# Norm 2 of a two-layer transformer trunk: four of the eight k tiles of the latent unit multiply tokens that the norm has not scaled yet

## The chip, the cores and the metric

The kernel runs on one core of a Trainium2 chip. Its metric is the device time in microseconds (us) of one execution; lower is better. One run is also recorded by the hardware profiler, and every row below comes from that recording. TensorE (PE) multiplies matrices, VectorE (DVE) and ScalarE (ACT) work on tiles in SBUF and PSUM, GpSimd (POOL) and SyncE (SP) mainly issue DMAs here.

## What is computed

Two layers over 256 tokens of width 1024. Each has a mixer (layer 0 sparse attention, layer 1 latent attention, MLA) and a gated feed-forward, and four times a root-mean-square norm stands between the residual stream x and a product:

```
mod = silu(c) @ ada_w[i] + ada_b[i]                  # shift, scale, gate of this layer
hm  = rms(x, norm_mix[i]) * (1 + scale) + shift      # norms 0 and 2
cq, ckv, k_rot = split(hm @ mla_w_in, [384, 640])    # layer 1: the "latent unit"
x   = x + gate * mixer(...)
hf  = rms(x, norm_ffn[i]) * (1 + scale_f) + shift_f  # norms 1 and 3
x   = x + gate_f * (silu(a) * b) @ ffn_w_out         # a, b = halves of hf @ ffn_w_in
```

Norm 2 is the one at the start of layer 1, between the down product of layer 0's feed-forward and the product with `mla_w_in`. Since a token's root is one number for all its columns, a product of normed tokens can be had as root times (x with gain and scale, times W), plus (shift times W), the same row for all tokens. That identity is what the change uses.

## The kernel before

Everything is one program per engine, with the order of the work written out by hand and semaphores between the engines. Tokens lie in T = 2 tiles of 128, the width in KD = 8 k tiles. A product in full precision is three matmuls, high by high, low weights by high tokens, high weights by low tokens (lines 1934 to 1936). So each weight slot s is loaded raw by SP, rounded by ACT into `w_hi` (`high`, line 778) and its rest is taken by DVE into `w_lo` (`low`, line 1165). A ring of RING = 4 slots is in use: slot s can be rounded when `slot_used` says that slot s - 4 was multiplied. `high_to(n)` and `low_to(n)` make all slots below n that are not made yet, in order. IN1 to IN1 + 3 are the four slots of the first latent unit (288 columns: key-value latent and rotary key), INB1 = IN1 + 4 to INB1 + 3 those of the second (384 columns: query latent). KVB1 is the first slot after them.

A norm in the old form, as norm 2 has it: DVE adds the gated down product into x in four pieces (two column halves, two token tiles; `update_x`, lines 1347 and 1355), ACT takes the squares of each (line 796), DVE makes the roots (lines 1202 to 1216) and scales both halves (`scaled_half`, line 1225). PE turns the scaled tokens in five batches (PIECES, line 1959), ACT applies scale and shift and rounds (lines 815 and 818: `st_hi`), DVE takes the rest (line 1241: `st_lo`), PE multiplies. While PE waits, `norm_start` has it multiply 42 and then 10 small filler matrices into a bank that nobody reads (line 2015, IDLE_FIRST and IDLE_SECOND).

Norms 1 and 3, ahead of the up products, already have the new form (`factored`, `early_tokens`, `first_unit`). There the first KU = 4 k tiles of x are turned before the root is known and kept in `early_hi`, `early_lo`; PE multiplies the shift row alone (`shift_hi`, `shift_lo`: the shift repeated for 128 tokens, into bank sc1) and then the early tokens; ACT copies the shift row's product; DVE folds root times early product plus shift row into `early_sums`. The other four k tiles go the old way as three batches (LATE_PIECES: tiles 4, 5, and 6 with 7), and DVE joins the two halves (line 1415). The tiles 0 to 3 are turned once more, scaled, as the last two batches of LATE_PIECES, since the following units need them in the old form.

After norm 2 DVE's list goes on as follows in both kernels: position to float (1768), angles (1771), then `low_to(KVB1)`, which makes the low parts of INB1 to INB1 + 3 if they aren't made yet, then the roots of the latents (1178 to 1196), their scaling (1793), and so on. PE's second latent unit waits for the low part of its slot before each slot.

## Time and profile before

| | us |
|---|---|
| median of 3 runs (733.5 to 735.42) | 733.95 |
| the profiled execution | 732.78 |
| its span, first to last instruction | 730.9 |
| PE busy in the span | 696.1 (95%) |
| DVE busy | 535.7 (73%) |
| ACT busy | 380.9 (52%) |
| last matmul of the down product starts | 416.17 |
| first matmul of the second latent unit starts | 432.22 |

A timeline row reads: start in us from the span's start, duration, engine, line, operation, output and inputs with shapes, how many instructions were merged, and in brackets how long the engine had stood idle and what released it. Matmuls overlap, so the distance of two starts is the pace and the duration is not. A "windows" row gives for a stretch its length, then the busy time of PE, of its weight loads, of DVE, ACT and POOL with instruction counts, the granted TensorE clock as a share of full speed, the DMA share and GB/s.

### The profile page before, as it was taken

How to read it: one execution, taken by the hardware profiler on the slowest of the kernel's cores; microseconds unless marked ns; L12 is line 12 of the kernel's file. 1: busy time of each engine (PE TensorE's matmuls, PEld its weight loads, DVE VectorE, ACT ScalarE, POOL GpSimd, SP SyncE). 2: the span in 40 equal slices, each digit the busy share in tenths (PEclk: the TensorE clock that was granted, in tenths of full speed). 3: DMA queues.
4: the chain of work that ended last, by engine and by line, in shares of the span. 5: the costliest groups of instructions: out<-in, count | busy, mean ns of one | idle time of the engine just before them, and what ended most of it. 6: DMA issues, size and time to landing. Idle time of an engine off the chain costs nothing. (4 is left out here: it accounts for less than half of the span.)

```text
span 730.9 us, 10691 instructions
## 1 busy us (share of the span) xinstructions
PE 696.1 (95%) x3839; PEld 569.7 (78%) x3839; DVE 535.7 (73%) x1004; ACT 380.9 (52%) x714; POOL 89.5 (12%) x175
## 2 busy tenths in 40 slices
PE   3799999999999999999999999889999999999997
PEld 2577768787778888878878887768888888878886
DVE  2356697999788989987887578978778765554444
ACT  2345566576468444444333379677576454444331
POOL 8020212000020111212211100600000000000000
PEclk9999999999999999999999999999999999999999
DMA  8997996033183999998898482601537865545621
GB/s 289 348 382 209 376 359 219 1 115 89 39 280 116 354 316 349 344 343 288 289 338 297 123 224 65 231 1 59 171 101 242 287 204 176 174 171 173 212 76 58
DMA packets 93742, 155.09 MB, mean 212 GB/s; under 512 B 5979, under 2 KB 68064, under 8 KB 93696
## 3 DMA queue, kind: packets, MB, share of 16 engines
q1 hardware_dynamic: 80768, 111.24, 45.9%
q0 software_dynamic: 12928, 43.24, 17.3%
q8 instruction: 28, 0.46, 0.3%
q14 instruction: 18, 0.15, 0.1%
HBM read 151.32 MB, written 1.05 MB: 208 GB/s over the span
## 5 line engine op out<-in xcount | busy, mean ns | idle before, releaser
L778 ACT ACTIVATE w_hi<-raw 128x1024 fp32r<-128x1024 f32 (+3 forms) x198 | 200.8, 1024 | 252.0 <-PE lin L1936 228.2
L1165 DVE TENSOR_TENSOR w_lo<-raw,w_hi 128x1024 fp32r<-128x1024 f32 (+3 forms) x198 | 233.0, 1186 | 110.6 <-ACT w_hi L778 110.0
L1934 PE MATMUL lin<-w_hi,st_hi 128*128 128x512 f32 (+2 forms) x552 | 220.0, 398 | 2.3 <-DVE w_lo L1165 2.0
L1936 PE MATMUL lin<-w_hi,st_lo 128*128 128x512 f32 (+2 forms) x552 | 212.6, 385 | 0.0
L1935 PE MATMUL lin<-w_lo,st_hi 128*128 128x512 f32 (+2 forms) x552 | 211.9, 384 | 0.0
L1934 PEld LDWEIGHTS lin<-w_hi,st_hi 128*128 128x128 f32 x552 | 104.1, 189 | 27.4 <-issue 5.2
L1936 PEld LDWEIGHTS lin<-w_hi,st_lo 128*128 128x128 f32 x552 | 103.9, 188 | 20.6
L1935 PEld LDWEIGHTS lin<-w_lo,st_hi 128*128 128x128 f32 x552 | 104.3, 189 | 18.6 <-issue 0.7
L634 POOL DMA_DIRECT2D ada_ring<-in_ada_w_dram x80 | 42.7, 534 | 384.0 <-DVE acc L1302 299.7
L1302 DVE SCALAR_TENSOR_TENSOR acc<-ada_ring,cond_b,acc 128x1024 f32<-128x1024 f32 x64 | 81.9, 1280 | 2.1 <-DMA ada_ring<-in_ada_w_dram 2.0
L1934 PE MATMUL lin<-w_hi,hid_hi 128*128 128x512 f32 x176 | 70.2, 399 | 0.2 <-DVE hid L1401 0.2
L1936 PE MATMUL lin<-w_hi,hid_lo 128*128 128x512 f32 x176 | 68.9, 392 | 0.0
L1935 PE MATMUL lin<-w_lo,hid_hi 128*128 128x512 f32 x176 | 68.5, 389 | 0.0
L1936 PEld LDWEIGHTS lin<-w_hi,hid_lo 128*128 128x128 f32 x176 | 33.0, 188 | 7.7
L1934 PEld LDWEIGHTS lin<-w_hi,hid_hi 128*128 128x128 f32 x176 | 33.1, 188 | 7.4 <-DVE hid L1401 0.6
L1935 PEld LDWEIGHTS lin<-w_lo,hid_hi 128*128 128x128 f32 x176 | 33.1, 188 | 7.2 <-issue 0.2
L866 ACT ACTIVATE z<-z,nmax 128x128 f32<-128x128 f32 x64 | 28.4, 445 | 14.3 <-DVE nmax L1378 14.3
L815 ACT ACTIVATE tfull<-tp,ada_cols,scale_cols 128x256 f32<-128x256 f32 x32 | 16.5, 557 | 12.3 <-issue 7.1
L1241 DVE TENSOR_TENSOR st_lo<-tfull,st_hi 128x512 fp32r<-128x512 f32 (+1 forms) x22 | 13.3, 607 | 12.2 <-ACT st_hi L818 11.9
L1347 DVE TENSOR_TENSOR scratch<-lin,gate_rows 128x512 f32<-128x512 f32 x16 | 11.0, 689 | 11.8 <-PE lin L1936 11.7
L1959 PE MATMUL tp<-ident,z 128*128 128x128 f32 x96 | 16.4, 281 | 3.4 <-ACT prob_t L874 3.4
L796 ACT ACTIVATE scratch<-x 128x512 f32<-128x512 f32 x16 | 10.0, 625 | 16.3 <-DVE x L1355 13.2
(295 smaller groups left out, 892.3 us busy)
## 6 DMA issues: line engine op xcount, KB each, us to landing
raw<-in_ffn_w_in_dram SPq DMA_DIRECT2D x88, 512.0 KB, 5.1
ada_ring<-in_ada_w_dram POOLq DMA_DIRECT2D x80, 512.0 KB, 6.2
raw<-in_ffn_w_out_dram SPq DMA_DIRECT2D x22, 1024.0 KB, 5.6
raw<-in_nsa_w_in_dram SPq DMA_DIRECT2D x10, 1024.0 KB, 12.7
ada_first<-in_ada_w_dram SPq DMA_DIRECT2D x8, 1024.0 KB, 13.0
raw<-in_nsa_cmp_w_dram SPq DMA_DIRECT2D x4, 1024.0 KB, 10.6
raw<-in_nsa_w_out_dram SPq DMA_DIRECT2D x4, 1024.0 KB, 9.6
raw<-in_mla_w_out_dram SPq DMA_DIRECT2D x4, 1024.0 KB, 5.5
```

Of the source, the lines that this page charges most:

```text
L634: pool.dma_start(ada_ring[:, n % ARING, :], ada_source(a)).then_inc(ada_landed[n % ARING], 16)
L778: nc.scalar.activation(part_of(w_hi, s), raw_part(s), ACT.Copy).then_inc(hi_ready, 1)
L815: ins = nc.scalar.activation(dst, src, ACT.Identity, scale=scale[:, k:k + 1], bias=shift[:, k:k + 1])
L866: e = nc.scalar.activation(prob_b[:, n % 3, c0:c0 + w], prob_b[:, n % 3, c0:c0 + w], ACT.Exp, bias=nmax[:, n % 4, t:t + 1], scale=-1.0, ac ...
L1165: nc.vector.tensor_tensor(part_of(w_lo, s), raw_part(s), part_of(w_hi, s).bitcast(F32), ALU.subtract).then_inc(lo_ready, 1)
L1241: nc.vector.tensor_tensor(low[:, k0:k0 + nk, :], tfull[:, m % 2, 0:nk * S].rearrange("p (k s) -> p k s", k=nk), high[:, k0:k0 + nk, :].bit ...
L1302: nc.vector.scalar_tensor_tensor(total, ada_ring[:, n % ARING, :], cond_b[:, kt, 0:1], total, ALU.mult, ALU.add).then_inc(acc_summed, 1)
L1347: ins = nc.vector.tensor_tensor(tmp, lin[2 * (unit % 2) + t][:], gate_rows[:, row, 512 * n:512 * n + 512], ALU.mult)
L1934: nc.tensor.matmul(bank, a_h, w_h, start=first, stop=False)
L1935: nc.tensor.matmul(bank, a_h, w_l, start=False, stop=False)
L1936: return nc.tensor.matmul(bank, a_l, w_h, start=False, stop=last)
L1959: ins = nc.tensor.transpose(tp[batch % 2][0:rows, n * P:(n + 1) * P], src, ident[:])
```

## The change

Norm 2 takes the form of norms 1 and 3. The fillers at norm 2 go. Buffers of its own (`mid_hi`, `mid_lo`, `mid_sum`) hold its shift, since the usual ones lie over a part of `hid_lo` that the last down products still read. The first latent unit becomes a shift product (12 matmuls of 288 columns), early products for tiles 0 to 3 (24) and late products for tiles 4 to 7 (24). Its sum is now written to `proj1` by DVE (the join), and ACT squares it there; ACT's two copies of this unit go. The low parts of IN1 and IN1 + 1 are moved into the middle of the last x update. POOL's two DMAs that fill the unused rows of the query and key tiles wait for the join and no longer for the down product, as they would write over the early tokens. The second latent unit waits for the last two batches of tokens. Norms 1 and 3 only change names.

```diff
-T_H1 = _batches(len(PIECES), "st")
+T_XM = _batches(2, "st")
+T_H1 = _batches(len(LATE_PIECES), "st")
...
-            pool.wait_ge(slot_used, IN1)
+            pool.wait_ge(halves_joined, 2 * T)
...
# ACT
-            before_norm(DOWN0 + FK, 2)
-            modulated(2, T_H1, 6)
+            shift_split(2, 6)
+            squares_of_x(2, 0)
+            high_to(IN1 + 2)
+            squares_of_x(2, 1, [0])
+            early_high(2, T_XM, 0)
+            squares_of_x(2, 1, [1])
+            early_high(2, T_XM, 1)
+            high_to(IN1 + 4)
+            modulated(2, T_H1, 6, LATE_PIECES, 0, 2)
+            shift_sum_copied(2, KVL + ROT)
+            modulated(2, T_H1, 6, LATE_PIECES, 2)
...
                     bank = lin[2 * ((U_IN1 + u) % 2) + t]
+                    if u == 0:
+                        act.wait_ge(halves_joined, T + t + 1)
+                        bank = proj1[:, t, c0:c0 + n]
...
-                    ev = nc.scalar.activation(proj1[:, t, c0:c0 + n], bank[:, 0:n], ACT.Copy)
+                    if u == 1:
+                        ev = nc.scalar.activation(proj1[:, t, c0:c0 + n], bank[:, 0:n], ACT.Copy)
...
# DVE
+            shift_low(2, 6)
             update_x(U_DOWN0, 1, 0, (part_done, 2))
-            update_x(U_DOWN0 + 1, 1, 1, (slot_used, DOWN0 + FK), 3)
-            low_to(DOWN0 + FK + 1)
-
-
-            normalise_x()
-            modulated(IN1)
+            update_x(U_DOWN0 + 1, 1, 1, (slot_used, DOWN0 + FK), 3, lambda: low_to(IN1 + 2))
+            early_low(0)
+            roots_of_x()
+            early_low(1)
+            factored(2, IN1, U_IN1, KVL + ROT)
+            for k0, nk in LATE_PIECES[3:]:
+                scaled_low(k0, nk)
+            dve.wait_ge(slot_used, INB1)
+            dve.wait_ge(early_folded, 2)
+            for t in range(T):
+                nc.vector.tensor_tensor(proj1[:, t, QL:MLA_IN], early_sums[t][:, 0:KVL + ROT],
+                                        lin[2 * (U_IN1 % 2) + t][:, 0:KVL + ROT], ALU.add).then_inc(halves_joined, 1)
...
# PE
+            def early_product(norm, unit0, s0, n, tp_x, t, k):
+
+                cols = slice(t * P, (t + 1) * P)
+                pe.wait_ge(resid, 4 * (norm - 1) + T + t + 1)
+                pe.wait_ge(st_ready, stationary_number(tp_x) + k // 2 + 1)
+                ins = half_product(lin[2 * ((unit0 - 1) % 2) + t], s0, n,
+                                   (early_hi[:, k, cols], early_lo[:, k, cols]), k, 0)
+                if t == T - 1 and k % 2 == 1:
+                    ins.then_inc(slot_used, 1)
+
+            def late_products(norm, unit0, s0, n, tp_h):
+
+                wait_unit(unit0)
+                for k in range(KU, KD):
+                    pe.wait_ge(lo_ready, s0 + k // 2 + 1)
+                    if k < KD - 1:
+                        pe.wait_ge(st_ready, stationary_number(tp_h) + k - KU + 1)
+                        x_batch(tp_h, k - KU + 2)
+                    for t, sides in enumerate(stationary(k)):
+                        ins = half_product(lin[2 * (unit0 % 2) + t], s0, n, sides, k, KU)
+                    if k % 2 == 1:
+                        ins.then_inc(slot_used, 1)
+                pe.wait_ge(early_folded, norm)
...
-            norm_start(T_H1, 10, IDLE_FIRST)
-            unit(U_IN1, IN1, FOUR, KVL + ROT, stationary, st_wait(T_H1, x_batch))
+            early_tokens(2, T_XM)
+            shift_product(2, IN1, KVL + ROT, 10)
+            for q in range(2):
+                for t in range(T):
+                    for k in (2 * q, 2 * q + 1):
+                        early_product(2, U_IN1, IN1, KVL + ROT, T_XM, t, k)
+            for m in range(2):
+                x_batch(T_H1, m)
+            late_products(2, U_IN1, IN1, KVL + ROT, T_H1)
...
             def key_value_latent(k):
 
+                if k in (0, 2):
+                    pe.wait_ge(st_ready, stationary_number(T_H1) + 4 + k // 2)
```

`factored` is unchanged but for its arguments: scale columns 512 to 1023 of x; low part of slot s + 2; rests of the batches with tiles 4 and 5; low part of slot s + 3; root; scale columns 0 to 511; wait for the shift row; fold; rest of the batch with tiles 6 and 7.

## Rows read from the trace of the kernel before

**Rows 1.** The page's first part: busy time, share of span, instructions.

```profile
PE 696.1 (95%) x3839; PEld 569.7 (78%) x3839; DVE 535.7 (73%) x1004; ACT 380.9 (52%) x714; POOL 89.5 (12%) x175
```

**Rows 2.** Windows view, from the down product's end to the second latent unit.

```profile
416.40:432.22 15.82, 14.54 (x117) 13.98 (x116) 12.27 (x29) 11.62 (x22) 2.16 (x2) 1.00 0.83 193
```

**Rows 3.** Timeline of PE at norm 2.

```profile
416.17 0.40 PE L1936 MATMUL lin<-w_hi,hid_lo 128*128 128x512 f32 x1
416.40 4.85 PE L2015 MATMUL sc<-ident,ones 128*128 128x128 f32 x42
...
424.14 0.38 PE L1934 MATMUL lin<-w_hi,st_hi 128*128 128x288 f32 x1
424.36 0.30 PE L1935 MATMUL lin<-w_lo,st_hi 128*128 128x288 f32 x1
424.49 0.29 PE L1936 MATMUL lin<-w_hi,st_lo 128*128 128x288 f32 x1
...
426.98 0.63 PE L1959 MATMUL tp<-ident,scratch 128*128 128x128 f32 x4 [0.55 <-DVE st_lo L1241]
...
432.22 0.34 PE L1934 MATMUL lin<-w_hi,st_hi 128*128 128x384 f32 x1
```

**Rows 4.** Timeline of DVE at norm 2.

```profile
411.10 0.69 DVE L1347 TENSOR_TENSOR scratch<-lin,gate_rows 128x512 f32<-128x512 f32 x1 [3.75 <-PE lin L1936]
...
426.14 0.69 DVE L1241 TENSOR_TENSOR st_lo<-tfull,st_hi 128x512 fp32r<-128x512 f32 x1 [1.07 <-ACT st_hi L818]
426.75 0.75 DVE L1165 TENSOR_TENSOR w_lo<-raw,w_hi 128x576 fp32r<-128x576 f32 x1
...
429.36 0.69 DVE L1241 TENSOR_TENSOR st_lo<-tfull,st_hi 128x512 fp32r<-128x512 f32 x1 [0.96 <-ACT st_hi L818]
...
430.58 3.68 DVE L1165 TENSOR_TENSOR w_lo<-raw,w_hi 128x768 fp32r<-128x768 f32 x4
```

**Rows 5.** Timeline of ACT at norm 2.

```profile
412.55 0.63 ACT L796 ACTIVATE scratch<-x 128x512 f32<-128x512 f32 x1 [7.69 <-DVE x L1355]
...
426.01 1.00 ACT L815 ACTIVATE tfull<-tp,ada_cols,scale_cols 128x256 f32<-128x256 f32 x2
...
427.64 1.02 ACT L815 ACTIVATE tfull<-tp,ada_cols,scale_cols 128x256 f32<-128x256 f32 x2
```

**Rows 6.** Timeline of PE at norm 1, which has the new form.

```profile
213.27 0.39 PE L1936 MATMUL lin<-w_hi,st_lo 128*128 128x512 f32 x1
...
218.79 0.50 PE L1934 MATMUL lin<-w_hi,early_hi 128*128 128x512 f32 x1
...
220.29 0.60 PE L1959 MATMUL tp<-ident,scratch 128*128 128x128 f32 x4
...
225.53 0.63 PE L1959 MATMUL tp<-ident,scratch 128*128 128x128 f32 x4
```

**Rows 7.** Timeline of DVE at norm 1.

```profile
221.81 0.43 DVE L1241 TENSOR_TENSOR st_lo<-tfull,st_hi 128x256 fp32r<-128x256 f32 x1 [1.15 <-ACT st_hi L818]
222.72 0.42 DVE L1241 TENSOR_TENSOR st_lo<-tfull,st_hi 128x256 fp32r<-128x256 f32 x1 [0.48 <-ACT st_hi L818]
223.06 1.22 DVE L1165 TENSOR_TENSOR w_lo<-raw,w_hi 128x1024 fp32r<-128x1024 f32 x1
...
224.39 0.88 DVE L1225 TENSOR_SCALAR scratch<-x,stat 128x512 f32<-128x512 f32 x2
225.19 0.74 DVE L1268 SCALAR_TENSOR_TENSOR silu_a<-lin,stat,shift_sum 128x512 f32<-128x512 f32 x1
```

**Rows 8.** Timeline of PE after the first pauses of the kernel.

```profile
21.16 1.09 PE L1959 MATMUL tp<-ident,scratch 128*128 128x128 f32 x4 [2.09 <-DVE st_lo L1241]
...
24.18 0.63 PE L1936 MATMUL lin<-w_hi,st_lo 128*128 128x512 f32 x1
24.61 0.57 PE L1934 MATMUL lin<-w_hi,st_hi 128*128 128x512 f32 x1
```

**Rows 9.** Timeline of PE at the start of the key-value product.

```profile
441.40 0.50 PE L1934 MATMUL lin<-w_hi,st_hi 128*128 128x512 f32 x1 [0.23 <-DVE st_lo L1241]
```

More of the change, by code:

```diff
@@ L1264, in factored @@
                 scaled_half(0)
[L1265 removed]
+                dve.wait_ge(shift_copied, norm)
                 dve.wait_ge(slot_used, s + 2)
                 for t in range(T):
[L1268 to L1269 removed]
+                    ins = nc.vector.scalar_tensor_tensor(
+                        early_sums[t][:, 0:n], lin[2 * ((unit - 1) % 2) + t][:, 0:n], root[:, t:t + 1],
+                        shifts[norm - 1][2][:, 0:n], ALU.mult, ALU.add)
                 ins.then_inc(early_folded, 1)
                 scaled_low(*LATE_PIECES[2])
[L1273 to L1279 removed]
             def low_from_tp(batch, hi, lo, i=None):
@@ L1915, in _ @@
             roots_of_x()
-            factored(1, UP1, U_UP1)
+            factored(3, UP1, U_UP1)
             def last_sums(u):
@@ L2015, in idle_into, with shift_product, half_product @@
                     nc.tensor.matmul(bank[:, 0:P], ones[:], ident[:], start=True, stop=True)
-            def norm_start(batch0, seg_read, n):
+            def shift_product(norm, s0, n, seg_read):
                 pe.wait_ge(ada_out, ada_at(seg_read))
-                idle_into(sc[1], n)
-                for m in range(2):
-                    x_batch(batch0, m)
-                idle_into(sc[1], IDLE_SECOND)
+                pe.wait_ge(shift_ready, norm)
+                hi, lo, _ = shifts[norm - 1]
+                for k in range(KU):
+                    pe.wait_ge(lo_ready, s0 + k // 2 + 1)
+                    ins = half_product(sc[1], s0, n, (hi[:, k, :], lo[:, k, :]), k, 0)
+                ins.then_inc(shift_done, 1)
+            def half_product(bank, s0, n, sides, k, first):
+                s, j = s0 + k // 2, k % 2
+                return three(bank[:, 0:n], *sides, w_hi[:, s % RING, n * j:n * j + n],
+                             w_lo[:, s % RING, n * j:n * j + n], k == first, k == first + KU - 1)
+            def early_product(norm, unit0, s0, n, tp_x, t, k):
[9 more added lines that the diff above has]
+                for k in range(KU, KD):
+                    pe.wait_ge(lo_ready, s0 + k // 2 + 1)
+                    if k < KD - 1:
[6 more added lines that the diff above has]
+                pe.wait_ge(early_folded, norm)
             def stationary(k):
@@ L2167, in feed_forward @@
                 hid0 = stationary_number(tp0)
[L2169 to L2172 removed]
                 def first_unit():
[L2176 to L2181 removed]
+                    shift_product(2 * layer + 1, up, 512, seg_read)
                     for t in range(T):
[L2183 to L2184 removed]
                         for k in range(KU):
[L2186 to L2190 removed]
+                            early_product(2 * layer + 1, unit0, up, 512, tp_x, t, k)
                         if t == 0:
@@ L2193, in first_unit @@
                                 x_batch(tp_h, m)
[L2194 to L2204 removed]
+                    late_products(2 * layer + 1, unit0, up, 512, tp_h)
                 def wait_st(k):
```

82 lines of the change are left out of this document (22 added, 60 removed).

## Prediction

> **What bounds the kernel now.** I read the page's first part, then the windows view around norm 2, then the timelines of PE, DVE and ACT there, and last those of norm 1, which already has the new form. PE is busy 95% of the span [rows 1], so outside its few pauses the kernel is as long as PE's work. Norm 2 is such a pause in disguise. The last down matmul starts at 416.17, and what follows at 416.40 are 42 filler matmuls that give nothing [rows 3]; the first useful product starts at 424.14 and the second latent unit at 432.22. Those 15.82 us hold 14.54 us of "busy" PE [rows 2], but 48 matmuls of 288 columns at a pace of 0.13 (424.36 to 424.49, [rows 3]) are only 6.4 us. The reader is to see that the rest is a chain through DVE, ACT and PE (x, squares, roots, scaling, turning, rounding, rest), and that what a change here is worth is read at one point: when the second latent unit can start.
>
> **What the change does to that chain.** Norm 1 is the ruler. Its last matmul starts at 213.27 [rows 6], that of norm 2 at 416.17, so I add 202.90 to norm 1's times as long as the work is the same, and correct where a slot has 576 columns and not 1024.
>
> Hidden at no cost: the shift's high and low parts (one ACT and one DVE instruction of 512 columns, each about the 0.63 and 0.69 of such tiles), because ACT stands idle 7.69 us before 412.55 [rows 5] and DVE 3.75 us before 411.10 [rows 4]; the 12 matmuls of the shift product (12 x 0.13 = 1.6 us), because PE has only fillers then; the low parts of IN1 and IN1 + 1, moved ahead of the last x update, which end when that update's product is there (they delay it by at most 0.1, and ACT, not DVE, is what the early tokens wait for). If that cover were gone, the two low parts would cost 2 x 0.75 [rows 4]. The ACT copies that go (two short ones) lie behind the join and aren't on the path to the second unit. POOL's two DMAs start some 16 us later; behind them on POOL stands only the rotation of queries, not due before the query unit, and SP's loads for later slots go out as the low parts are made.
>
> Now step by step:
> 1. PE's second group of early products starts at 218.79 + 202.90 = 421.69 [rows 6]. It has 12 matmuls, 0.22 for the first (424.14 to 424.36) and 0.13 for the others, 1.7 us in all [rows 3]: end 423.38. Here the shorter product is no help yet; PE turns the late tiles 4 and 5 at 423.38.
> 2. In norm 1 the rests of these two batches start 1.52 and 2.43 us after the turning at 220.29 [rows 6, 7]: 424.90 and 425.81.
> 3. From the second of them to the scaling of columns 0 to 511 norm 1 takes 224.39 - 222.72 = 1.67, which has a low part of 1.22 in it [rows 7]; here that low part takes 0.75 [rows 4], so 1.20: DVE scales at 427.01. That is the first new delay: the old kernel had both halves scaled in one go, before any turning. PE turns tiles 0 and 1 at 225.53 - 224.39 = 1.14 later [rows 6, 7]: 428.15.
> 4. ACT follows a turning after 427.64 - 426.98 = 0.66 [rows 3, 5]: 428.81; its next batch of two tiles comes 427.64 - 426.01 = 1.63 later [rows 5]: 430.44. The turning for that one (tiles 2 and 3) waits for the rest of tiles 6 and 7, which DVE makes after scaling (0.80, [rows 7]) and two folds. A fold of 288 columns has no row: at least what I take for the join below (0.37), at most the 0.74 of 512 columns [rows 7]; nearer to the first for its width, 0.43. The rest starts at 427.01 + 0.80 + 2 x 0.43 = 428.67 and the turning 426.98 - 426.14 = 0.84 after it [rows 3, 4], at 429.51, 0.3 ahead of what ACT needs (430.44 - 0.66). So ACT's pace decides, barely; with the dear folds the batch would come 0.35 later.
> 5. DVE's last rest starts 429.36 - 427.64 = 1.72 after ACT [rows 4, 5]: 432.16. In the old kernel it is at 429.36. That is 2.80 late, though the unit itself is done earlier: after that turning (four matrices at the fillers' pace of 4.85 / 42 = 0.115, [rows 3]) PE has 12 matmuls left and ends at 429.51 + 0.46 + 0.09 + 12 x 0.13 = 431.6, 0.6 before 432.22.
> 6. Then comes the new wait. **Nobody has made the low part of INB1.** The old list goes from the last rest at 429.36 to the low part at 430.58, 1.22 in all [rows 4]: the rest, the cast and the angles. The first of the four low parts takes 0.95 (3.68 in four, the last one whole), ready at 431.53, and PE got there at 432.22: a slack of 0.54 with 0.15 for the signal (426.98 - 426.14 - 0.69). The new list has the join in between. The trace shows no join of 288 columns. The nearest rows are rests of 256 columns (0.34 from start to next start, 222.72 to 223.06, [rows 7]) and of 512 (0.61, 426.14 to 426.75, [rows 4]); I take 0.37 each, close to the first: 0.74 for both, at most 1.22. It doesn't wait itself, as PE is done at 431.6.
> 7. So the low part of INB1 starts at 432.16 + 1.22 + 0.74 = 434.12, is there at 435.07, and PE starts the second unit at 435.22 in place of 432.22. **Sum: + 2.80 + 0.74 - 0.54 = + 3.00 us.** PE stands still from about 431.7 to 435.2. Queued behind the wait on PE are the second unit, the turned key-value latent and the key-value product; behind the join on DVE are the four low parts, the latent's roots and its scaling.
>
> By the Trainium skill ("VectorE: DVE Perf Modes", section on the TRN2 errata), an operand in PSUM has a fixed cost of 120 cycles and not 58, which would make the two joins 0.13 us longer, + 3.1 instead of + 3.0; the trace shows no such difference between a fold from PSUM (0.74) and other tiles of 512 columns beyond 0.05 [rows 4, 7].
>
> **Does it stay?** Later pauses of PE end on DVE and ACT work that itself hangs on this unit: the key-value product starts at 441.40 after a wait of 0.23 for a rest of the latent [rows 9], which hangs on the turning inside the second unit. DVE's own list moves by 2.80 + 0.74 = 3.5 up to the low parts, and what follows on it waits for the same unit's squares and turnings. All three engines move together, and loads are released by low parts, with no fixed date. Nothing gives it back.
>
> **Rivals.**
> A, as above: + 3.0. Its own range: the step 4 tie, the join's bounds (0 to + 0.5), and 0.5 for the ruler: + 2.2 to + 3.9. Chance 0.62.
> B, the clock falls. With the fillers gone PE pauses some 1.7, 1.3 and 3.5 us in 12 us. For it: after the kernel's first pauses (2.09 us before 21.16) matmuls of 512 columns start 0.43 apart (24.18 to 24.61), against 0.23 at norm 2 (416.17 to 416.40), so these ran at 1.2 GHz and not at 2.4 [rows 3, 8]. Against it: the slow stretch lies at the very start, the pauses to come follow 400 us of steady work, and the granted clock at norm 2 is 1.00 now [rows 2]. Price: slow from 21.16 to 24.61 [rows 8], 3.45 us x (1 - 0.23 / 0.43) loses 1.6. Total + 4.6, up to + 5.5 if it falls twice. The Trainium skill ("TensorE: Matmul & The Clock Gate", section "Why this matters for your kernels") tells one to leave no longer idle gaps between bursts of matmuls, since the clock falls back; by that rule this would be the likely case, and no row after the start shows it. Chance 0.20.
> C, the low part of INB1 doesn't bind, because DVE and ACT fall behind less than the ruler says. Then PE's own end at 431.6 sets the start: - 0.6. Chance 0.12, with cases where later slack takes the loss in.
> D, faster. The late products wait for no rest at all, PE runs through from 423.38: 16 matrices turned (1.8) and 24 matmuls (3.1 and 0.4 for starts), end 428.7, - 3.5 us. It decides only if tiles 0 and 1 are scaled before about 425; step 3 has 427.01. Chance 0.06.
>
> **How the numbers follow.** Forecast A: the profiled execution from 732.78 to 735.8 (span 730.9 to 733.9); the median of the runs lies 1.17 above that execution, so 733.95 + 3.0 = 736.95. Range: from A's low end less a little (735.6) to B with its second fall nearly whole (739.2). Under it lie C and D, 0.18. About 0.3% (2.2 us) is what a measurement can tell from no change: A lies below that in 0.05 of cases, so same = 0.12 + 0.05 = 0.17, slower = 0.57 + 0.20 = 0.77, faster = 0.06.
>
> **What would show it.** PE: no fillers, the first early products near 419.3, the turning of tiles 0 and 1 near 428.2, the last late product near 431.6, and a pause of some 3.5 us before the first matmul of 384 columns, ended by the low part of INB1 (line of `low`). DVE: the join right behind the last rest, near 432.8. If the second unit starts before 433, steps 3 to 6 are wrong; if matmuls after the pause start 0.32 apart and not 0.17, B is right.

## Result, and the profile of the changed kernel

The changed kernel takes 738.46 us (median of 7 executions, 737.01 to 741.46) against 733.95 for the kernel before (7 executions, 731.95 to 735.42). The two medians differ by 4.51 us; the ratio, estimated from all executions, is 1.0074, 95% interval 1.0055 to 1.0093: **slower by 4.0 to 6.8 us**, where + 3.0 was forecast. Run twice more, the unaltered kernel gave 1.0061 (1.0037 to 1.0085) and 1.0059 (1.0040 to 1.0079), so 4.3 to 5.4 us is what has to be explained.

The profiled execution of the changed kernel took 738.07 us; its span is 736.3 (730.9 before). The page's first part, to be laid beside [rows 1]:

```profile
PE 695.2 (94%) x3807; PEld 568.2 (77%) x3807; DVE 539.0 (73%) x1012; ACT 384.0 (52%) x720; POOL 89.3 (12%) x175
```

PE has 32 instructions fewer (52 fillers and the old unit's 48 matmuls against 60 and eight more turned matrices), while DVE works 3.3 us more and ACT 3.1 us more. The new form takes fillers from PE, which cost nothing there, and gives work to the two engines that PE waits for.

Timeline of PE at norm 2, in the changed kernel (columns as in the rows of before; `lin` is the unit's bank, `tp` turned matrices):

```profile
417.30 0.39 PE L1946 MATMUL lin<-w_hi,hid_lo 128*128 128x512 f32 x1
...
420.54 0.37 PE L1944 MATMUL lin<-w_hi,early_hi 128*128 128x288 f32 x1 [0.39 <-DVE early_lo L1250]
...
422.92 0.37 PE L1944 MATMUL lin<-w_hi,early_hi 128*128 128x288 f32 x1 [0.55 <-DVE early_lo L1250]
...
424.58 0.60 PE L1969 MATMUL tp<-ident,scratch 128*128 128x128 f32 x4
426.78 0.63 PE L1969 MATMUL tp<-ident,scratch 128*128 128x128 f32 x4 [1.60 <-DVE st_lo L1250]
427.16 0.38 PE L1944 MATMUL lin<-w_hi,st_hi 128*128 128x288 f32 x1
427.38 0.29 PE L1945 MATMUL lin<-w_lo,st_hi 128*128 128x288 f32 x1
427.50 0.29 PE L1946 MATMUL lin<-w_hi,st_lo 128*128 128x288 f32 x1
...
429.35 1.09 PE L1969 MATMUL tp<-ident,scratch 128*128 128x128 f32 x4 [1.16 <-DVE scratch L1234]
430.09 0.59 PE L1944 MATMUL lin<-w_hi,st_hi 128*128 128x288 f32 x1
430.47 0.44 PE L1945 MATMUL lin<-w_lo,st_hi 128*128 128x288 f32 x1
430.71 0.44 PE L1946 MATMUL lin<-w_hi,st_lo 128*128 128x288 f32 x1
...
431.67 1.04 PE L1969 MATMUL tp<-ident,scratch 128*128 128x128 f32 x4
...
434.02 0.29 PE L1946 MATMUL lin<-w_hi,st_lo 128*128 128x288 f32 x1
437.63 0.41 PE L1944 MATMUL lin<-w_hi,st_hi 128*128 128x384 f32 x1 [3.32 <-DVE w_lo L1174]
...
446.90 0.50 PE L1944 MATMUL lin<-w_hi,st_hi 128*128 128x512 f32 x1 [0.21 <-DVE st_lo L1250]
```

Two things are to be seen. Besides the two waits of 0.39 and 0.55 us ahead of the early products there are three longer pauses, 1.60, 1.16 and 3.32 us, and the last is ended by the low part of INB1, in place of 432.22 with no pause in [rows 3]. And the late products of one batch start 0.13 apart (427.38 to 427.50), those of the next 0.24 apart (430.47 to 430.71). The windows view says why (the third number from the end is the granted clock):

```profile
428.00:429.00 1.00, 0.19 (x2) 0.00 (x0) 0.96 (x4) 0.97 (x3) 0.00 (x0) 1.00 0.00 0
429.00:430.00 1.00, 0.65 (x3) 0.68 (x4) 1.00 (x4) 0.18 (x1) 0.00 (x0) 0.58 0.54 143
430.00:431.00 1.00, 1.00 (x7) 1.00 (x6) 0.54 (x1) 0.53 (x2) 0.00 (x0) 0.50 0.82 274
432.00:433.00 1.00, 1.00 (x8) 1.00 (x7) 0.69 (x1) 0.40 (x2) 0.00 (x0) 0.71 0.62 246
433.00:434.00 1.00, 1.00 (x9) 1.00 (x9) 0.00 (x0) 0.97 (x3) 0.00 (x0) 1.00 0.05 21
```

From about 429 to 432.6 PE runs at 1.2 GHz and not at 2.4. Timeline of DVE in the changed kernel:

```profile
426.10 0.42 DVE L1250 TENSOR_TENSOR st_lo<-tfull,st_hi 128x256 fp32r<-128x256 f32 x1 [1.86 <-ACT st_hi L822]
...
428.20 0.88 DVE L1234 TENSOR_SCALAR scratch<-x,stat 128x512 f32<-128x512 f32 x2
429.00 0.51 DVE L1278 SCALAR_TENSOR_TENSOR silu_a<-lin,stat,mid_sum 128x288 f32<-128x288 f32 x1
429.43 0.51 DVE L1278 SCALAR_TENSOR_TENSOR hid<-lin,stat,mid_sum 128x288 f32<-128x288 f32 x1
429.86 0.69 DVE L1250 TENSOR_TENSOR st_lo<-tfull,st_hi 128x512 fp32r<-128x512 f32 x1
...
434.47 0.69 DVE L1250 TENSOR_TENSOR st_lo<-tfull,st_hi 128x512 fp32r<-128x512 f32 x1 [1.59 <-ACT st_hi L822]
435.08 0.45 DVE L1764 TENSOR_TENSOR proj<-silu_a,lin 128x288 f32<-128x288 f32 x1
435.45 0.45 DVE L1764 TENSOR_TENSOR proj<-hid,lin 128x288 f32<-128x288 f32 x1
...
436.42 3.56 DVE L1174 TENSOR_TENSOR w_lo<-raw,w_hi 128x768 fp32r<-128x768 f32 x4
```

And one row of its timeline of ACT:

```profile
430.47 1.02 ACT L819 ACTIVATE tfull<-tp,ada_cols,scale_cols 128x256 f32<-128x256 f32 x2 [1.29 <-PE tp L1969]
```

**The ruler of the comparison.** The last down matmul starts at 417.30 here and at 416.17 before. PE's work up to there is the same in both, and over the runs below that start lies anywhere from 415.19 to 419.25. So every time of norm 2 is told below from the start of that matmul: the second unit starts at + 20.33 here and at + 16.05 before, the key-value product at + 29.60 (446.90) and at + 25.23 (441.40, [rows 9]). The change costs **4.37 us at the key-value product**. Nothing comes back later: the next four pauses of PE end at 453.25, 454.47, 464.05 and 467.81, before at 447.76, 448.99, 458.59 and 462.33, 5.46 to 5.49 apart, which is 4.37 and the 1.13 of the start.

### The profile page after: what moved, and what is told of

Read it like the earlier page. It is cut to its first block, busy times and chain, and to the rows that moved or that the text cites. A ratio compares the mean times of both kernels' runs of the same rounds, so it can differ in the third digit from the quotient of the medians.

```text
span 736.3 us, 10670 instructions
## 1 busy us (share of the span) xinstructions
PE 695.2 (94%) x3807; PEld 568.2 (77%) x3807; DVE 539.0 (73%) x1012; ACT 384.0 (52%) x720; POOL 89.3 (12%) x175
## 4 chain that ended last, share of the span: by engine, by line
PE 80%; DVE 7%; ACT 5%; issue 3%; DMA 3%; SPq 2%; DVEq 0%
PE lin L1944 22%; PE lin L1946 22%; PE lin L1945 21%; PE tp L1969 5%; DMA raw<-in_nsa_w_in_dram 2%; SPq L552 2%; PE tp L2251 1%; PE sc L2109 1%; DMA ada_ring<-in_ada_w_dram 1%; ACT z L870 1%; PE sc L2160 1%; PE sc L2151 1%; PE sc L2175 1%; PE lin L2201 1%; PE lin L2202 1%
## 5 line engine op out<-in xcount | busy, mean ns | idle before, releaser
L782 ACT ACTIVATE w_hi<-raw 128x1024 fp32r<-128x1024 f32 (+3 forms) x198 | 200.5, 1023 | 252.7 <-PE lin L1946 229.1
L1944 PE MATMUL lin<-w_hi,st_hi 128*128 128x512 f32 (+1 forms) x544 | 218.3, 401 | 5.6 <-DVE w_lo L1174 5.3
L1946 PE MATMUL lin<-w_hi,st_lo 128*128 128x512 f32 (+1 forms) x544 | 210.7, 387 | 0.0
L1945 PE MATMUL lin<-w_lo,st_hi 128*128 128x512 f32 (+1 forms) x544 | 210.1, 386 | 0.0
L870 ACT ACTIVATE z<-z,nmax 128x128 f32<-128x128 f32 x64 | 28.4, 445 | 14.4 <-DVE nmax L1381 14.4
L1969 PE MATMUL tp<-ident,scratch 128*128 128x128 f32 x65 | 12.5, 322 | 6.4 <-DVE st_lo L1250 5.2
```

What stands on the lines that cost most here:

```text
L782: nc.scalar.activation(part_of(w_hi, s), raw_part(s), ACT.Copy).then_inc(hi_ready, 1)
L870: e = nc.scalar.activation(prob_b[:, n % 3, c0:c0 + w], prob_b[:, n % 3, c0:c0 + w], ACT.Exp, bias=nmax[:, n % 4, t:t + 1], scale=-1.0, ac ...
L1944: nc.tensor.matmul(bank, a_h, w_h, start=first, stop=False)
L1945: nc.tensor.matmul(bank, a_h, w_l, start=False, stop=False)
L1946: return nc.tensor.matmul(bank, a_l, w_h, start=False, stop=last)
L1969: ins = nc.tensor.transpose(tp[batch % 2][0:rows, n * P:(n + 1) * P], src, ident[:])
```

## Experiments

**Theory O (order):** the loss is DVE's list, the late scaling and the low part of INB1 behind the join, as forecast. **Theory K (clock):** the lost fillers let the clock fall. Measures are the start of the second unit and of the key-value product from the start of the last down matmul, the ratio, and the mean granted clock that each execution has with it. "Under 0.999" counts the executions whose mean clock is below that; the kernel before has such ones too (12 of 25 beside e1 to e4, 15 of 23 beside e5 to e7 and the second run of the changed kernel, 6 of 17 beside e8, 6 of 15 beside e9 and e10, 10 of 23 beside e11 and e12), since in five of the profiles below the clock falls between 20 and 42 us as well. The count thus says that the clock fell somewhere, not that it fell at norm 2, and even beside each other programs differ in it for other reasons: e3 has no such execution in ten, though it changes nothing ahead of norm 2. Where it falls can be read only in the profiles.

| kernel | second unit | key-value product | ratio (interval) | clock under 0.999 |
|---|---|---|---|---|
| before | + 16.05 | + 25.23 | | see above |
| changed | + 20.33 | + 29.60 | 1.0074 (1.0055 to 1.0093) | 7 of 7 |
| changed, again | + 20.18 | + 32.04 | 1.0061 (1.0037 to 1.0085) | 4 of 4 |
| changed, third | + 19.16 | + 29.97 | 1.0059 (1.0040 to 1.0079) | 6 of 6 |
| e1 low parts early | + 15.44 | + 26.37 | 1.0013 (0.9998 to 1.0027) | 4 of 10 |
| e11 the same again | + 16.63 | + 26.82 | 1.0022 (1.0007 to 1.0036) | 10 of 12 |
| e2 too many fillers | + 21.95 | + 31.20 | 1.0074 (1.0046 to 1.0102) | 2 of 4 |
| e3 e1 and fillers | + 16.69 | + 27.70 | 1.0021 (1.0006 to 1.0036) | 0 of 10 |
| e4 before, no fillers | + 17.74 | + 26.91 | 1.0018 (1.0005 to 1.0031) | 10 of 10 |
| e5 scaling early | + 18.27 | + 29.08 | 1.0072 (1.0050 to 1.0093) | 4 of 4 |
| e6 all pauses covered | + 18.84 | + 28.10 | 1.0030 (1.0017 to 1.0044) | 5 of 10 |
| e7 three edits | + 15.00 | + 25.93 | 1.0000 (0.9986 to 1.0014) | 5 of 12 |
| e8 best order | + 14.85 | + 25.71 | 1.0001 (0.9985 to 1.0016) | 6 of 12 |
| e9 short pauses covered | + 19.00 | + 31.06 | 1.0055 (1.0037 to 1.0074) | 10 of 10 |
| e10 long pause covered | + 20.88 | + 30.16 | 1.0059 (1.0041 to 1.0077) | 6 of 6 |
| e12 the same again | + 20.17 | + 29.43 | 1.0042 (1.0024 to 1.0060) | 7 of 12 |

### e1: the low parts of INB1 and INB1 + 1 in DVE's gaps

```diff
# ACT
-            modulated(2, T_H1, 6, LATE_PIECES, 2)
+            modulated(2, T_H1, 6, LATE_PIECES, 2, 3)
+            high_to(INB1 + 1)
+            modulated(2, T_H1, 6, LATE_PIECES, 3, 4)
+            high_to(INB1 + 2)
+            modulated(2, T_H1, 6, LATE_PIECES, 4)
# DVE
-            for k0, nk in LATE_PIECES[3:]:
+            for m, (k0, nk) in enumerate(LATE_PIECES[3:]):
+                low_to(INB1 + 1 + m)
                 scaled_low(k0, nk)
```

> The changed kernel with one move: ACT rounds and DVE takes the low parts of INB1 and INB1 + 1 in the gaps between the last three batches of tokens, ahead of the join. Theory 1 (the order of DVE's list makes the pause of 3.3 us before the second latent unit): the pause goes, the second unit starts within 0.3 us of the last late product; PE then catches DVE's later roots, so about 2.8 us of the loss come back and the kernel is 1 to 2.5 us slower than before. Theory 2 (the pause is a symptom of something else, the join or the clock): the pause stays above 2 us and the time is that of the changed kernel, 4.5 to 5.5 us slower than before. The slow stretch of TensorE during the late products (granted clock 0.50 for about 3 us) should stay in both.

Measured: DVE makes the two low parts while it waits for ACT's batches, and PE goes from the late products into the second unit without a pause. Timeline of DVE of e1, then that of PE:

```profile
432.41 0.95 DVE L1178 TENSOR_TENSOR w_lo<-raw,w_hi 128x768 fp32r<-128x768 f32 x1
433.73 0.69 DVE L1254 TENSOR_TENSOR st_lo<-tfull,st_hi 128x512 fp32r<-128x512 f32 x1 [0.37 <-ACT st_hi L822]
434.46 0.96 DVE L1178 TENSOR_TENSOR w_lo<-raw,w_hi 128x768 fp32r<-128x768 f32 x1
```

```profile
434.56 0.30 PE L1951 MATMUL lin<-w_hi,st_lo 128*128 128x288 f32 x1
434.69 0.33 PE L1949 MATMUL lin<-w_hi,st_hi 128*128 128x384 f32 x1
```

The second unit starts 4.89 us earlier than in the changed kernel and even 0.61 earlier than before. Theory 1 holds: the pause goes, the key-value product gains 3.23 (2.8 was said), and the kernel is 1.0 us slower than before (from 0.1 faster to 2.0 slower). The slow stretch, which was expected to stay, did not: the granted clock is 1.00 at norm 2 in this profile, so the fair measure is e6 below, which has the changed order with the clock held: from e6 to e1 the second unit gains 3.40 (18.84 to 15.44) and the key-value product 1.73 (28.10 to 26.37), of the 2.87 that the order costs. So the wait that the forecast named is the larger part of that loss; 1.14 stay. They arise on DVE, which is busy without a wait from the last rest (+ 16.79) to the latent's roots (+ 20.47, before + 18.82).

### e2 and e3: fillers, twice as many as meant

```diff
 # PE, late_products (e2 and e3)
+                        if norm == 2 and k < KU + 2:
+                            idle_into(sc[0], (12, 8)[k - KU])
                         pe.wait_ge(st_ready, stationary_number(tp_h) + k - KU + 1)
 # PE, behind late_products(2, ...) (e2 alone; e3 has the edits of e1 instead)
+            idle_into(sc[0], 24)
```

> The changed kernel with filler matmuls put back into the pauses of PE: 12 before the turning of tiles 6 and 7, 8 before the turning of tiles 0 and 1, 24 after the last late product. Nothing else moves. Theory 1 (the clock falls because PE pauses at norm 2): granted clock 1.00 all through norm 2, the last batch of tokens 1.0 to 1.3 us earlier, time 1.2 to 3 us below the changed kernel, near 3.0 us slower than before, and less spread between runs. Theory 2 (the clock's fall costs nothing, since PE waits anyway): time as the changed kernel.

> Both edits together (no fillers after the last late product, as no pause should be left there). If order and clock are two separate causes, the gains add: about 4 to 5 us below the changed kernel, within 0.3% of before or slightly faster. If they are one cause, it is no better than the better of the two alone.

Measured: the helper makes two instructions of 0.115 us for each one asked for, so e2 has 24, 16 and 48 of them. The last group ran 5.52 us and held the second unit up itself (+ 21.95). e2 therefore says only that the clock is held (1.00 throughout norm 2; the profile has falls elsewhere, one at 470.6 to 474), not what it is worth, and its forecast of about 3.0 us over before was missed. In e3 the fillers overrun the short pauses too: the key-value product is 1.33 later than in e1. It is within 0.3% of before, as was said, but no faster than e1 (1.0021 and 1.0013): whether the two gains add is not shown by it. The lesson is used in e6.

### e4: the kernel before without its 52 fillers

```diff
-IDLE_FIRST, IDLE_SECOND = 21, 5
+IDLE_FIRST, IDLE_SECOND = 0, 0
```

> The kernel before without its 52 filler matmuls at norm 2, nothing else. If the fall of the clock comes from taking the fillers away and not from the new form, the clock falls here too and the time is 1 to 4 us above before. If the new form's own pattern makes it fall, the time is that of before, as PE only waits there.

Windows view of e4, then two rows of its timeline of PE:

```profile
418.00:427.00 9.00, 5.04 (x22) 4.69 (x23) 6.33 (x18) 4.98 (x11) 0.06 (x1) 0.50 0.97 172
```

```profile
424.17 0.44 PE L1935 MATMUL lin<-w_lo,st_hi 128*128 128x288 f32 x1
424.41 0.44 PE L1936 MATMUL lin<-w_hi,st_lo 128*128 128x288 f32 x1
```

Without fillers PE pauses for 4.99 and 1.39 us here. The clock is at 1.2 GHz for these nine microseconds, the matmuls of 288 columns are 0.24 apart, and the key-value product is 1.68 late; the ratio of 1.0018 is 1.3 us, within the 1 to 4 that were said. All ten executions are under 0.999. So the fillers of the old kernel were not free to take away: the forecast had them as work that gives nothing. The pause of 4.99 us is not one of the changed kernel, though, which has products in that place and a granted clock of 1.00 there.

### a1 and a2: the changed kernel unaltered

> The changed kernel unaltered, on the same chip as the next three, for comparison. From the last down matmul to the first matmul of the key-value product it took 29.60 us in its first profile against 25.23 before, 4.37 more, of which 1.2 is a fall of the clock that need not come again: 28.4 to 29.7 here, and a time 0.4 to 0.8% above before.

> The changed kernel itself, unaltered, beside the two versions with one pause covered. Both theories expect a mean granted clock near 0.994 and a ratio of 1.006 to 1.0075; the rows say in which pause it falls this time.

Windows view of a1, then that of a2:

```profile
429.00:432.00 3.00, 3.00 (x15) 2.98 (x14) 1.50 (x3) 1.71 (x4) 0.00 (x0) 0.50 0.92 309
...
436.00:442.00 6.00, 5.18 (x16) 5.21 (x17) 5.66 (x19) 2.69 (x10) 1.54 (x2) 0.50 0.82 112
```

```profile
430.00:436.00 6.00, 3.22 (x25) 2.88 (x23) 3.86 (x10) 5.60 (x10) 0.66 (x1) 1.00 0.47 169
...
437.00:440.00 3.00, 3.00 (x10) 3.00 (x11) 2.86 (x9) 0.75 (x6) 0.52 (x1) 0.50 1.00 142
```

One program, three profiles, three places: the first fell ahead of the long pause, a1 ahead of it and again in it (the second unit's matmuls 0.32 apart and the key-value product at + 32.04, where 28.4 to 29.7 was said), a2 at the end of the long pause alone. That is why one profile doesn't price a fall, and why the count of executions is in the table: 17 of 17 of the changed kernel are under 0.999, against 21 of 38 of the kernel before beside the last ten of them.

### e5: both halves scaled before the late batches

```diff
                 scaled_half(512)
+                if norm == 2:
+                    scaled_half(0)
                 low_to(s + 3)
...
-                scaled_half(0)
+                if norm != 2:
+                    scaled_half(0)
```

> The changed kernel with one move: DVE scales columns 0 to 511 right after columns 512 to 1023, in the pause it has anyway while the first late batches are turned and rounded. Theory 1 (the last batch of tokens is late because these columns are scaled late): the turning of tiles 0 and 1 follows the products of tile 4 without a wait, the last rest comes 0.7 to 1.2 us earlier, and so does the second latent unit; time 0.8 to 1.5 us below the changed kernel. Theory 2 (ACT's pace of 1.63 us a batch decides alone): no change beyond 0.3 us.

Measured: the second unit starts at + 18.27, 0.57 earlier than in e6 below, which has the late scaling and a held clock, and the last rest at + 15.12 and not + 15.84. The turning of tiles 0 and 1 follows the products of tile 4 without a wait, as theory 1 said. The late scaling alone is thus worth some 0.6 to 0.7 us at the second unit. In this profile the clock fell as the long pause ended (0.50 from 437.5 to 440.9), and the key-value product starts at + 29.08. The gain in time that was forecast (0.8 to 1.5 us) doesn't show: ratio 1.0072 from four executions.

### e6: the order as changed, all three pauses covered

```diff
+                        if norm == 2 and k < KU + 2:
+                            idle_into(sc[0], (6, 4)[k - KU])
                         pe.wait_ge(st_ready, stationary_number(tp_h) + k - KU + 1)
...
+            idle_into(sc[0], 13)
```

> The changed kernel with half as many fillers as in the run before (12, 8 and 26 small matmuls; each call of the helper makes two, so that run had twice what was meant and held PE up). Theory 1 (clock and order are separate): granted clock 1.00 all through norm 2 and a stretch of 28.2 to 28.5 us from the last down matmul to the key-value product, that is 3.0 to 3.3 more than before, 0.40 to 0.45% in time, below the changed kernel. Theory 2 (the clock's fall costs nothing): 29.6 us again.

Windows view of e6 from the down product to the second unit, then its timeline of PE:

```profile
418.40:437.24 18.84, 17.16 (x133) 15.97 (x131) 13.70 (x35) 14.97 (x31) 1.27 (x2) 1.00 0.35 113
```

```profile
433.84 3.06 PE L2025 MATMUL sc<-ident,ones 128*128 128x128 f32 x26
...
437.24 0.41 PE L1944 MATMUL lin<-w_hi,st_hi 128*128 128x384 f32 x1 [0.34 <-issue]
```

This is the changed kernel with the clock taken out of it: granted clock 1.00 throughout norm 2, key-value product + 28.10 (28.2 to 28.5 was said), which is **+ 2.87 against before**, ratio 1.0030 (+ 1.2 to + 3.2 us). The forecast, case A, was + 3.00. What separates it from the changed kernel (+ 1.5 in the first profile, + 3.9 in a1, + 1.9 in a2; 0.0029 to 0.0044 in the ratios) is theory K. Beside each other stand e6 and a1, with 1.0030 (up to 1.0044) and 1.0061 (from 1.0037): the intervals just touch, so the rows carry this reading more than the times do.

### e9 and e10: which pause does it?

Each has one half of the edit of e6.

```diff
 # e9
+                        if norm == 2 and k < KU + 2:
+                            idle_into(sc[0], (6, 4)[k - KU])
                         pe.wait_ge(st_ready, stationary_number(tp_h) + k - KU + 1)
 # e10
             late_products(2, U_IN1, IN1, KVL + ROT, T_H1)
+            idle_into(sc[0], 13)
```

> The changed kernel with small matmuls in its two short pauses only: 12 ahead of the turning of tiles 6 and 7 (pause 1.60 us) and 8 ahead of that of tiles 0 and 1 (1.16 us); the long pause behind the late products (3.3 us) stays open. It asks which pause makes the clock fall. Theory L (the long one, in most executions, though the fall of the changed kernel's profile began ahead of it): the mean granted clock of the executions stays near 0.994 as in the changed kernel (0.9943 over 11 executions, 0.998 in the kernel before), the key-value product starts 28 to 32 after the last down product's start, ratio 1.006 to 1.007. Theory S (the short ones): mean clock near 0.998, key-value product at 28.1, ratio 1.003.

> The changed kernel with 26 small matmuls behind the late products only, which cover the long pause of 3.3 us; the two short pauses (1.60 and 1.16 us) stay open. Theory L (the long pause makes the clock fall in most executions): mean granted clock near 0.998, ratio 1.003. Theory S (the short pauses do): mean clock near 0.994 to 0.996, the late products at 0.24 and not 0.13 apart in the profile, key-value product near 29.6, ratio 1.005 to 1.007.

Timeline of PE of e9 and its windows view, then the same of e10:

```profile
435.67 0.66 PE L1944 MATMUL lin<-w_hi,st_hi 128*128 128x384 f32 x1 [3.41 <-DVE w_lo L1174]
```

```profile
436.00:440.00 4.00, 4.00 (x14) 4.00 (x14) 3.66 (x14) 0.69 (x6) 0.41 (x1) 0.50 1.00 140
```

```profile
428.89 1.09 PE L1969 MATMUL tp<-ident,scratch 128*128 128x128 f32 x4 [1.15 <-DVE scratch L1234]
```

```profile
428.00:434.00 6.00, 5.11 (x23) 5.13 (x24) 2.77 (x6) 3.99 (x9) 0.00 (x0) 0.50 0.54 175
```

Neither theory of the two expectations wins alone. With the short pauses covered the profile has a fall in the long one (434.8 to 441.6, key-value product + 31.06), and all 10 executions are under 0.999; with the long one covered the profile has a fall that starts in the second short pause (428.0 to 434.8, + 30.16), and all 6 are under; the kernel before has 6 of 15. Either was enough in its profile, and of the profiles in the changed order the clock is held at norm 2 only where both are covered (e6, and e2).

### e11 and e12: does e1's order spare the clock?

e1 has the two short pauses open as well and had shown no fall. It was run again, beside e10 again.

> The version with the low parts of INB1 and INB1 + 1 made early, unaltered, beside the version with only the long pause covered by small matmuls. Both have the same two short pauses open (1.60 and 1.16 us) and no long one. If the short pauses make the clock fall in this version too, it has a mean granted clock near 0.994 this time, late products 0.24 apart, and a ratio of 1.003 to 1.004 (the earlier 1.0013 was then luck or another chip's habit). If the order itself spares it, the mean clock is near that of the kernel before (0.997 to 0.998) and the ratio again 1.001.

> The version with 26 small matmuls in the long pause only, unaltered, on the same chip as the version with the low parts made early. Expected from its first runs: mean granted clock near 0.994, every execution below 0.999, ratio near 1.006. If it holds near 0.998 here, the fall in the short pauses is a matter of the chip or of chance and not of the kernel.

Windows view of e11, then that of e12:

```profile
428.00:431.00 3.00, 2.56 (x12) 2.58 (x13) 2.50 (x5) 2.35 (x5) 0.00 (x0) 0.50 0.77 240
```

```profile
429.00:431.00 2.00, 2.00 (x11) 1.98 (x10) 0.86 (x2) 1.18 (x3) 0.00 (x0) 0.50 0.93 311
```

This time e1's order fell too (10 of 12 under 0.999, where the kernel before had 10 of 23), and of e10's only 7 of 12 are under 0.999, where every one was expected to be; ratio 1.0042, not 1.006. The order doesn't spare the clock, and five executions of e12 lack a fall as long as those of the profiles, though the short pauses are open: whether it falls there differs from execution to execution. Those five, at 0.999 or more, have a median of 734.93, the 7 below 737.97. This isn't the price of a fall at norm 2, because the kernel before, beside it, has 2.1 of these 3.0 us between its own two kinds: 732.96 and 735.06. The price is read at the key-value product, against the + 28.10 of e6: 1.3 to 2.1 us for a fall that starts in the short pauses (e12, changed, e10), 1.9 and 3.0 for one in the long pause (a2, e9), 3.9 for both (a1). In e11's order it costs less (26.82 against 26.37), since DVE's list is what ends last there. What decides in which execution the clock falls was not found.

### e7 and e8: can the new form win?

e7 is e1 and e5 together, with the cast and the angles (lines 1778 and 1781) ahead of the last two rests and 12 small matmuls in the first pause.

```diff
             for m, (k0, nk) in enumerate(LATE_PIECES[3:]):
                 low_to(INB1 + 1 + m)
+                if m == 0:
...
+                    link(nc.vector.tensor_copy(pos_f, pos_i[:]))
...
                 scaled_low(k0, nk)
...
+                            idle_into(sc[0], (6, 0)[k - KU])
```

> Everything that the runs point to at once: low parts of INB1 and INB1 + 1 in the gaps, both halves scaled in one go, cast and angles moved ahead of the join, and 12 fillers in the one pause that is left. The first of these alone left 1.14 us over before (26.37 against 25.23). The others should take 0.6 (angles) and 0.7 to 1.2 (scaling) from DVE's list: 24.6 to 25.1 us, 0.1% faster than before or the same. If the new form had an unavoidable cost beyond order, it would stay at 26 or more.

Measured: the second unit starts at + 15.00 and the key-value product at + 25.93, 0.8 later than the latest that was forecast and 0.70 later than before; the ratio is 1.0000 (0.9986 to 1.0014).

e8 goes further:

```diff
 # ACT
-            high_to(IN1 + 4)
+            high_to(INB1 + 1)
 # DVE, factored
+                if norm == 2:
+                    scaled_half(0)
+                    low_to(s + 4)
                 for k0, nk in LATE_PIECES[:2]:
                     scaled_low(k0, nk)
-                low_to(s + 4)
+                low_to(s + (5 if norm == 2 else 4))
 # DVE, behind factored: cast and angles, then
+            for k0, nk in LATE_PIECES[3:]:
+                scaled_low(k0, nk)
+            low_to(INB1 + 2)
             dve.wait_ge(slot_used, INB1)
...
 # PE
+                            idle_into(sc[0], (5, 0)[k - KU])
```

> The changed kernel with five edits at norm 2 together: ACT makes the high part of INB1 before the late batches; DVE makes the low parts of IN1 + 3 and of INB1 while it waits for ACT's batches; both column halves of x are scaled in one go, as in the old form; the cast, the angles and the low part of INB1 + 1 are done ahead of the last two rests, the join behind them; 10 small matmuls cover PE's pause before tile 4. Theory (the new form is slow only through the order of DVE's list and the lost fillers): the last late product starts about 14.8 after the last down product's start (15.3 to 16.7 in the kernels so far), the key-value product at 24.8 against 25.23 of the kernel before, ratio 0.999 to 1.000. Rival (DVE's list is simply too full in the new form: join, folds, two shift tiles and five early or late rests more, whatever their order): the key-value product stays at 25.9 as in the version with three of these edits, ratio 1.000 to 1.001, and no order of this form beats the old kernel.

Timeline of PE in e8, then those of DVE and of POOL, and last a row of DVE in e1:

```profile
430.86 0.34 PE L1949 MATMUL lin<-w_hi,st_hi 128*128 128x384 f32 x1
...
441.72 0.50 PE L1949 MATMUL lin<-w_hi,st_hi 128*128 128x512 f32 x1 [0.40 <-DVE st_lo L1250]
```

```profile
433.53 1.82 DVE L1174 TENSOR_TENSOR w_lo<-raw,w_hi 128x768 fp32r<-128x768 f32 x2
435.26 0.80 DVE L1187 TENSOR_SCALAR stat<-stat 128x2 f32<-128x2 f32 x2
```

```profile
435.01 1.09 POOL L748 DMA_DIRECT2D k_t<-ident  x1
```

```profile
439.72 0.23 DVE L1191 TENSOR_SCALAR stat<-stat 128x2 f32<-128x2 f32 x2
```

The second unit starts 1.20 earlier than before (+ 14.85), and it is worth nothing: the key-value product waits for a rest of the latent, whose roots DVE starts at + 19.25 (+ 18.82 before) and scales with 2.63 later (2.07 before). It starts at + 25.71, 0.48 late, and the ratio is 1.0001. The rival of its expectation (DVE's list is too full in whatever order) was nearer: 25.9 was said by it, 24.8 by the theory. None of these versions beats the old kernel; e7 and e8 equal it within 0.16%.

The rows hold a second reason, though. The first two instructions of the roots, 128 by 2 elements each, take 0.80 us together in e8 (0.16 and 0.73, overlapping) and 0.23 in e1, and the second of them ends when POOL's second DMA issue does (436.06 and 435.01 + 1.09 = 436.10). In e7 it is the same: 0.80, from 435.67 to 436.47, with POOL's issue until 436.50. In e1, e3 and e11 POOL's issue is over when the pair ends, and the pair takes 0.23. In the new form these issues wait for the join, and in the orders of e7 and e8 they fall on the roots. The 0.57 lost there is more than the 0.48 by which e8's key-value product is late; without it that product would start at about + 25.14 by an estimate from these rows, if nothing else ends later. No run moves the issues, so it stays open whether the length of DVE's list alone keeps the new form from winning.

## Why the prediction was right or wrong

The sign was right. The size was short: + 3.0 forecast, 4.0 to 6.8 measured, and 4.3 and 4.5 in the repeats. The median of the executions, 738.46, lies inside the range of 735.6 to 739.2; by the ratio the kernel is at 739.4, just past its upper end. The step that failed is the choice between A and B: the sum of + 3.00 has no term for TensorE's clock, and the runs show 1.5 to 3.9 us for it on top of an order that costs 2.87. Step by step, from the last down matmul (forecast times less 416.17):

| step | forecast | changed | e6, clock held |
|---|---|---|---|
| 1, second early group | 5.52 | 5.62 | 5.61 |
| 2, rests of tiles 4 and 5 | 8.73, 9.64 | 8.80, 9.70 | 8.79, 9.69 |
| 3, columns 0 to 511 scaled | 10.84 | 10.90 | 10.90 |
| 3, turning of tiles 0 and 1 | 11.98 | 12.05 | 11.88 |
| 4, rest of tiles 6 and 7 | 12.50 | 12.56 | 12.55 |
| 4, turning of tiles 2 and 3 | 13.34 | 14.37 | 13.38 |
| 5, last rest | 15.99 | 17.17 | 15.84 |
| 6, low part of INB1 | 17.95 | 19.12 | 17.78 |
| 7, second unit | 19.05 | 20.33 | 18.84 |
| key-value product | 28.23 | 29.60 | 28.10 |

**Steps 1 to 3 held** within 0.1 us: norm 1 was a good ruler, and the late scaling is the first new delay, as said.

**Step 4 failed, for one reason: the clock.** Its fold was right (429.00 to 429.43 is 0.43), and so was the rest. But the four matrices of tiles 0 and 1 took 1.09 and not 0.60, so ACT could start only at 430.47, after 1.29 of waiting for PE. The six late products behind them ran 0.24 apart and not 0.13, and pushed the next turning from 13.34 to 14.37. The forecast had said that ACT's pace decides barely; with the slow clock PE decides, and the 1.18 us at the last rest are nearly all of the 1.28 by which step 7 is late. With the clock held (e6) every step comes out within 0.21.

**Steps 5 to 7 held as mechanisms.** The pause was forecast as about 3.5 us, ended by the low part of INB1, and is 3.32 so ended. The joins were taken at 0.37 each from 0.34 for 256 columns: measured 435.08 to 435.45, 0.37. By the Trainium skill ("VectorE: DVE Perf Modes", section on the TRN2 errata) an operand in PSUM would have added 0.13 us to the two, by an estimate from its cycles; these rows don't show it. From the last rest to the low part it takes 436.42 - 434.47 = 1.95, where 1.22 + 0.74 = 1.96 was said. e1 shows by removal that this wait is the larger part of the order's loss (1.73 of 2.87).

**The choice between A and B was wrong.** Rival B (the clock falls, + 4.6 to + 5.5) is what the median shows; it had 0.20. It was argued down with the granted clock of 1.00 at norm 2 and 400 us of steady work ahead. But that 1.00 was read in a kernel whose fillers held it, and e4 shows what it is without them, with a pause of 4.99 us: 0.50 for nine microseconds. The 400 us of steady work ahead didn't hold it either: it fell in each of the three profiles of the changed kernel. **So the term that failed is the clock, put at nothing in the sum** (its pauses of some 1.7, 1.3 and 3.5 us were listed, and costed at full clock). What took the fillers' place is not at fault: the shift product was costed at nothing "because PE has only fillers then", and its 12 matmuls did run hidden, with the granted clock at 1.00, from 418.33 to 420.0, ahead of the early products, which wait for DVE until 420.54. The price of B was mis-sized little: 1.6 a fall said, 1.5 and 1.9 in the profiles of the changed kernel with one fall (28.10 to 29.60 and to 29.97), 3.9 in a1 with two. It came from rows whose slowness only the pace shows: from 21 to 25 us the windows view of the kernel before has a granted clock of 1.00, while the matmuls are 0.43 apart. Where it was placed was half right: around the first two pauses or the long one, by execution. The mark given for B, matmuls of the second unit 0.32 apart behind the pause, is absent in the first profile (437.88 to 438.06) and there in a1 (437.59 to 437.91) and a2 (437.24 to 437.56): a mark in one place was too narrow.

By the Trainium skill ("TensorE: Matmul & The Clock Gate", section "Why this matters for your kernels") idle gaps between bursts let the clock fall back. The traces agree: the clock fell in or at the end of the pause of 3.1 to 3.6 us in four profiles. It also fell in five profiles at the second of two pauses of 1.60 and 1.16 us (in it, or within 0.2 us of its end), with six matmuls of 288 columns between the two, though not in every execution.

**"Nothing gives it back"** held (5.46 to 5.49 at each later pause). **Rival C** (the low part of INB1 doesn't bind) is wrong: 3.32 us of waiting. **Rival D** (late products wait for nothing) is wrong: tiles 0 and 1 were scaled at + 10.90, and even e5, which scales them in one go, turns tiles 6 and 7 no earlier (+ 9.46). **POOL's DMAs** went out at 436.19, right behind the join, 18.2 us later after the last down matmul than before (416.86), where 16 was said. Nobody waited for them in the changed kernel; in e7 and e8 they meet DVE's roots.

The whole, then: 2.87 us for the order of DVE's list (1.73 of them go when the low parts are moved; moving the scaling alone brings the second unit 0.57 forward), and 1.5 to 3.9 us, by profile, for the clock.

## What to carry to other kernels

Removing fillers is a change of its own with a price; read it from a stage that has pauses and no fillers, or bound it by the granted clock halved over the stretch, never at zero because "the clock is 1.00 there now". When a product is split so that PE starts earlier, list what the engine that ends last gets in addition (here the rests of the shift and of the early tokens, folds and joins on DVE, whose busy time grew by 3.3 us) and ask which of its later items PE now waits for. And if a change opens pauses, look at several executions: the clock falls in some and not in others, and one profile shows only one of them. A mean clock over the execution doesn't say where it fell, so compare it with the kernel before, run beside it.

## What the runs showed of the hardware

- With pauses of 1.60 and 1.16 us between products of 288 columns PE fell to 1.2 GHz in five profiles (changed, a1, e10, e11, e12) and not in two (a2, e1). With a pause of 3.1 to 3.6 us it fell in it or as it ended in four (a1, a2, e5, e9) and not in one (the first).
- A fall lasted some 3.5 us in the changed kernel (429 to 432.6), 6.8 in e10 (428 to 434.8) and 10.2 in e4 (417.4 to 427.6).
- Executions of one program differ in it: e12 had 5 of 12 at 0.999 or more.
- Two small DVE instructions (tensor_scalar, 128 by 2 elements) took 0.80 us in place of 0.23 in the two profiles where a DMA issue of POOL ran beside them (e7, e8), and ended as it ended. Two profiles show it, no run was made for it.
- A full-precision filler of 128 columns shows as two instructions, 0.115 us each (26 in 3.06 us for 13 asked for).
- Covering the three pauses (6.1 us in all) with fillers that end in time brought the ratio from about 1.006 to 1.003; fillers that held the second unit up by 3.1 us (18.84 to 21.95) cost about as much as the fall that they prevented (e2: 1.0074 from four executions; key-value product + 31.20, against + 29.60 to + 32.04 in the changed kernel).
